# Gates' cumulative sums by split decay logarithms in single-pass products, in a two-layer hybrid token mixer on Trainium2

## What is computed

```python
def gla_chunked(q, k, v, logg, s0, with_output=True):
    g = jnp.cumsum(logg.astype(f32).reshape(b, n, GLA_CHUNK, h, dk), axis=2)
    g_last = g[:, :, -1]
    k_upd = k * jnp.exp(g_last[:, :, None] - g)
    ...
    g_mid = g[:, :, GLA_CHUNK // 2 - 1][:, :, None]
    scores = jnp.einsum('bnihd,bnjhd->bnhij', q * jnp.exp(g - g_mid), k * jnp.exp(g_mid - g))
    scores = jnp.where(mask, scores, 0.0)
    o_intra = jnp.einsum('bnhij,bnjhv->bnihv', scores, v)
    o_inter = jnp.einsum('bnihd,nbhdv->bnihv', q * jnp.exp(g), s_start)

logg_f = jax.nn.log_sigmoid((lr_f @ w_dec_f + b_dec_f).astype(jnp.float32)) / GLA_TAU
```

## Time and profile before

| | |
|---|---|
| median of 3 runs | 1604.45 us (1604.32 to 1606.06) |
| profiled execution | 1607.49 us, its span 1605.7 us, mean granted clock 0.988 |
| TensorE busy | 1541.2 us, 96% of the span |
| VectorE, ScalarE, GpSimd busy | 862.1, 569.0, 594.3 us |
| loop over the tiles, layer 0 | 263.3 to 310.3 us of the span |
| loop over the tiles, layer 1 | 1131.3 to 1166.0 us |

### The profile page before, as it was taken

The page is one execution under the profiler, slowest core; times in us unless marked ns, Lnnn a source line. Parts: engine busy times, 40 slices in busy tenths (PEclk is TensorE's granted clock), DMA queues, the critical chain, the costliest instruction groups (busy, mean ns, idle before and its releaser), DMA issues.

```text
span 1605.7 us, 22916 instructions
## 1 busy us (share of the span) xinstructions
PE 1541.2 (96%) x9056; PEld 1388.4 (86%) x9056; DVE 862.1 (54%) x1316; ACT 569.0 (35%) x916; POOL 594.3 (37%) x309
## 2 busy tenths in 40 slices
PE   5999999999999999999999979999999999999997
PEld 2899999886799999999999858888898888888887
DVE  2576888536646425761466675477756332223237
ACT  4644214426444213441244246432535321322221
POOL 0532211245324524553255223322342444444441
PEclk9999999999999999999999999999999999999999
DMA  9554531355312203122122341563130333323221
GB/s 369 200 167 153 162 125 59 113 173 206 118 52 81 79 26 104 54 79 79 53 80 64 140 162 54 196 198 116 51 136 27 118 108 116 130 91 103 93 83 61
DMA packets 54062, 183.93 MB, mean 115 GB/s; under 512 B 5650, under 2 KB 10642, under 8 KB 51028
## 3 DMA queue, kind: packets, MB, share of 16 engines
q1 hardware_dynamic: 47826, 168.85, 31.3%
q10 hardware_dynamic: 6146, 13.83, 2.5%
HBM read 171.13 MB, written 11.53 MB: 114 GB/s over the span
## 4 chain that ended last, share of the span: by engine, by line
PE 89%; DVE 5%; ACT 2%; DMA 1%; issue 1%; SPq 1%; POOL 1%; ACTq 0%; DVEq 0%; POOLq 0%
PE A L1038 62%; PE A L1292 8%; PE N L1292 4%; PE G L1292 4%; DMA raw<-modw 1%; PE A L1226 1%; PE A L1220 1%; PE G L1195 1%; PE G L1347 1%; PE G L1154 1%; PE A L1188 1%; DVE x L2177 1%; PE N L1138 1%; SPq L892 1%; DVE A L2176 1%
## 5 line engine op out<-in xcount | busy, mean ns | idle before, releaser
L976 POOL TENSOR_TENSOR w_lo<-raw,w_hi 128x1024 fp32r<-128x1024 f32 (+2 forms) x163 | 386.7, 2375 | 654.7 <-ACT w_hi L1374 617.4
L1038 PE MATMUL A<-h_hi,w_hi 128*128 128x512 f32 (+2 forms) x1264 | 414.6, 359 | 15.8 <-POOL h_lo L1021 7.0
L1038 PE MATMUL A<-h_lo,w_hi 128*128 128x512 f32 (+2 forms) x1264 | 405.2, 351 | 0.0
L1038 PE MATMUL A<-h_hi,w_lo 128*128 128x512 f32 (+2 forms) x1264 | 405.1, 351 | 0.0
L1374 ACT ACTIVATE w_hi<-raw 128x1024 fp32r<-128x1024 f32 (+2 forms) x163 | 167.5, 1030 | 372.6 <-PE A L1038 334.5
L1038 PEld LDWEIGHTS A<-h_hi,w_hi 128*128 128x128 f32 x1264 | 235.7, 190 | 55.2 <-issue 12.4
L1038 PEld LDWEIGHTS A<-h_hi,w_lo 128*128 128x128 f32 x1264 | 237.8, 191 | 22.1
L1038 PEld LDWEIGHTS A<-h_lo,w_hi 128*128 128x128 f32 x1264 | 237.8, 191 | 21.6 <-issue 0.5
L1038 PE MATMUL A<-g_hi,w_hi 128*128 128x384 f32 (+2 forms) x480 | 146.9, 349 | 3.8 <-DVE g_lo L1867 2.0
L1038 PE MATMUL A<-g_hi,w_lo 128*128 128x384 f32 (+2 forms) x480 | 145.8, 347 | 0.0
L1038 PE MATMUL A<-g_lo,w_hi 128*128 128x384 f32 (+2 forms) x480 | 145.8, 346 | 0.0
(11 more groups left out here) (313 smaller groups left out, 2625.6 us busy)
## 6 DMA issues: line engine op xcount, KB each, us to landing
raw<-stream SPq DMA_DIRECT2D x150, 512.0 KB, 3.7
mraw<-modv SPq DMA_DIRECT2D x54, 512.0 KB, 4.5
mraw<-modw SPq DMA_DIRECT2D x10, 1024.0 KB, 6.6
raw<-pairs SPq DMA_DIRECT2D x18, 512.0 KB, 4.8
raw<-modw SPq DMA_DIRECT2D x6, 1024.0 KB, 14.7
x<-x_keep ACTq DMA_DIRECT2D x4, 1536.0 KB, 13.7
raw<-stream SPq DMA_DIRECT2D x16, 384.0 KB, 3.1
bg<-modv SPq DMA_DIRECT2D x10, 512.0 KB, 3.8
```

The lines of the kernel that those rows point to most:

```text
L976: pool.tensor_tensor(lo, like_chunk(n, raw[:, n % RAW, 0:WIDTH[n]]), hi.bitcast(F32), ALU.subtract).then_inc(lo_done, 1)
L1038: m = pe.matmul(dst[:, at:at + t1 - t0], a, b[:, k, t0:t1], start=(first and p == 0), stop=(last and p == 2))
```

## The change

The decay logarithms are split too. For each tile ScalarE copies `ls` to `ls_high` in float32r, GpSimd subtracts to get `ls_low`, and `gate` becomes two single-pass products into one sum, `ls_high` and `ls_low` each with `mat_r`, a float32r copy of the constants (made once). There is one buffer of each. The new tensors lie over tensors that are not in use then (`wd`, the first part of `mat`, `mrow`), so all others keep their places. ScalarE makes the first tile's copy ahead of the `four` copies and each further one behind the exponentials of the tile before. GpSimd's subtraction for the next tile stands at this tile's gates, and the weight conversions are placed around it.

The pieces of the diff, in this order: allocation, GpSimd, TensorE at `gate`, ScalarE at `four`, ScalarE at `gate` behind its exponentials.

```diff
+        with ls_low_t:
+            ls_low = sb("ls_low", [P, 512], F32R, stack=ls_low_t)
...
+        with mat_t:
+            mat_r = sb("mat_r", [P, 4 * P], F32R, stack=mat_t)
...
+        with ls_high_t:
+            ls_high = sb("ls_high", [P, 512], F32R, stack=ls_high_t)
...
+                if e[0] == "gate":
+                    tiles = tiles_of(e[1])
+                    at = tiles.index(e[2])
+                    if at == 0 and e[3] == 0:
+                        low_until(PLAN.n0[e] + RING)
+                    elif e[3] and at:
+                        low_until(max(done[0], PLAN.n0[e] + (at if e[1] else max(0, at - 2))))
+                    if at + e[3] < len(tiles) and (e[3] or at == 0):
+                        pool.wait_ge(lshi_ready, nth(e[1], tiles[at + e[3]]) + 1)
+                        pool.tensor_tensor(ls_low[:, :], ls[:, tiles[at + e[3]], :], ls_high[:, :].bitcast(F32),
+                                           ALU.subtract).then_inc(lslo_ready, 1)
                 if e[0] == "fold":
-                    low_until(PLAN.n0[("wout", e[1])])
+                    low_until(max(done[0], PLAN.n0[("wout", e[1])]))
...
-                    read_out(pe, ("z", L, tt))
+                    pe.wait_ge(lslo_ready, nth(L, tt) + 1)
                     for pr in range(2):
-                        m = pe.matmul(G[g][:, pr * 256:(pr + 1) * 256], ls[:, tt, g * KW + pr * P:g * KW + (pr + 1) * P],
-                                      mat[:, g * 256:(g + 1) * 256], start=True, stop=True)
+                        own = slice(g * KW + pr * P, g * KW + (pr + 1) * P)
+                        pe.matmul(G[g][:, pr * 256:(pr + 1) * 256], ls_high[:, own], mat_r[:, g * 256:(g + 1) * 256],
+                                  start=True, stop=False)
+                        m = pe.matmul(G[g][:, pr * 256:(pr + 1) * 256], ls_low[:, own], mat_r[:, g * 256:(g + 1) * 256],
+                                      start=False, stop=True)
...
+                    if nth(L, tt) == 0:
+                        act.wait_ge(consts_in, 16 * 4)
+                        link(act.activation(mat_r[:, :], mat[:, 0:4 * P], ACT.Copy))
+                    if tt == tiles_of(L)[0]:
+                        for t in tiles_of(L):
+                            read_out(act, ("z", L, t))
+                        act.activation(ls_high[:, :], ls[:, tt, :], ACT.Copy).then_inc(lshi_ready, 1)
...
+                    at = tiles_of(L).index(tt) + 1
+                    if g and at < len(tiles_of(L)):
+                        act.activation(ls_high[:, :], ls[:, tiles_of(L)[at], :], ACT.Copy).then_inc(lshi_ready, 1)
```

More of the change, by code:

```diff
@@ L544, in bass_hybrid_block @@
         par = sb("par", [P, DEPTH * PCOLS + 16])
+        ls_low_t, mat_t, ls_high_t = ExitStack(), ExitStack(), ExitStack()
+        with ls_low_t:
+            ls_low = sb("ls_low", [P, 512], F32R, stack=ls_low_t)
         wd = sb("wd", [97, 512])
         mask = sb("mask", [P, 2, P], I32)
+        with mat_t:
+            mat_r = sb("mat_r", [P, 4 * P], F32R, stack=mat_t)
         mat = sb("mat", [P, 4 * P + 2 * P + 2])
@@ L657, in bass_hybrid_block @@
         qk_ready, r_scaled = sem("qk_ready"), sem("r_scaled")
+        lshi_ready, lslo_ready = sem("lshi_ready"), sem("lslo_ready")
         osq_ready, orstd_ready, yg_ready, yhi_ready, ylo_ready = (
```

## The result

The change made the kernel slightly slower: 1607.99 us median (20 runs) against 1605.26 us for the kernel before in the same comparison (20 runs). The ratio is 1.0016, 95% interval 1.0010 to 1.0023, that is +2.6 us (+1.6 to +3.7): the ratio lies within the 0.2% that were called "same" ahead, its interval reaches 0.23%. Predicted were +2.15 (+0.5 to +4.5) and 1606.6 us; of the 1.4 us between that and 1607.99, 0.8 come from the median of the kernel before, which stood at 1604.45 after three runs and stands at 1605.26 after twenty.

A forecast was written before the change was run, and what follows sets the result against it. Layer 0 was taken as bound by two nearly equal chains, TensorE's 7.79 us and a ScalarE-VectorE loop of 7.6; layer 0's +3.15 and layer 1's -1.0 summed to +2.15, 1606.6 us, range +0.5 to +4.5.

The forecast's parts named there:

- The lock between VectorE and GpSimd: GpSimd's subtraction runs between VectorE's two products of a tile, making the second 1.15 later in every tile but the last.
- Layer 0, tile by tile: Layer-0 loop: shifts of each tile's first exponential, -1.15, then +1.15, +1.0, +1.15, +1.0, summing to +3.15 us.
- Tile 2: earlier by one and a half gates: Layer 0, second tile's first exponential: comes 1.15 us earlier through the cheaper gates.
- Layer 1: Layer-1 loop: first two tiles about even; third has 2.3 - 1.15 less in VectorE's way, of which -1.0 us is kept.
- Gates: TensorE's gates: eight single-pass products take 0.95 instead of 1.73 us, saving 0.78 per tile, 7.8 us of queue over ten tiles.
- gates not cheaper: Rival: gate products cost 0.216 per pair-of-types product, so layer 0 +4.7, layer 1 -0.7, total +4.0, 1608.5 us; chance 0.04.
- TensorE's idle of 1.7 us: Layer 0, each of the last three tiles: TensorE idle some 1.7 us (8.75 - 7.01) before score or mean-square products.
- no collision: Rival: subtraction slips in before or beside VectorE's first product; layer 0 gains 1.1, layer 1 2.3, giving 1601.0 us; chance 0.11.

The follow-up runs named there:

- e5: Kernel after, with GpSimd's subtraction, from the third tile's logarithms on, waiting until VectorE's two products of the current tile are done; ratio 1.0008.
- e4: Kernel before, with only layer 1's first output-projection weight conversion on GpSimd moved early, to the second tile's gate; ratio 0.9986.
- e1: Kernel after without GpSimd's ten subtractions, each second gate product repeating the rounded half, so the low part is left out; ratio 0.9989.
- e2: Kernel after with the float32 gates of before, the subtraction kept and waited for though unread, ScalarE's copy of the constants left out; ratio 1.0017.
- e7: Kernel after with subtractions from the third tile on moved to VectorE, and ScalarE's square behind the weight conversion in some tiles; ratio 0.9994.
- e10: Kernel before with layer 1's early weight conversion, the square behind the conversion, and GpSimd's second layer-1 conversion held back; 1603.74 us, ratio 0.9997.
- e11: Kernel after with subtractions from the third tile on VectorE, the later square, and GpSimd's second layer-1 weight conversion held back; ratio 1.0002.

## Why the prediction held, point by point

The mechanism, a subtraction that takes its turn between VectorE's two products, came as predicted. The size came right in part by luck: in each layer two terms were too large, one of them a gain and one a price, and their errors nearly cancel.

- **The lock between VectorE and GpSimd: right in kind and size.** Taken were 1.15 to 1.2 for the subtraction, between the two products; measured is 1.14 (295.79 - 294.65), and L2049 at 1.75. The Trainium skill (SBUF — State Buffer, "Who interferes with whom") says that two-input VectorE work and GpSimd's reads shut each other out for whole instructions; e5 shows it in one tile, where the product with a PSUM input ran through at 0.68 and the one with two SBUF inputs took 1.33.
- **Layer 0, tile by tile.** The first exponentials stand at 265.71, 273.66, 282.42, 291.04 and 299.65, in before at 265.60, 272.53, 280.54, 288.11 and 295.90. Counted from the first `four` product, against before: tile 2 -0.39, tile 3 +0.63, tile 4 +1.38, tile 5 +2.43, tile 6 +3.25, end +3.35. Predicted: -1.15, 0, +1.0, +2.15, +3.15. The end is right through **two errors that cancel**. The step that failed is "Tile 2: earlier by one and a half gates": the first tile's gates gave nothing, since the DFT products behind them wait for the last low part of the `four` stage (255.34 in after, again 6.95 us behind the first `four` product, 0.55 us idle). And each later tile added less than said: +1.02, +0.75, +1.05, +0.82 instead of +1.15, +1.0, +1.15, +1.0.
- **Layer 1:** predicted -1.0, measured -0.83. But its parts were mis-sized, and again the errors cancel. Taken were 2.3 for the conversion moved away and 1.15 back for the subtraction, both in the third tile; the early conversion alone gives 1.44 (e4), and the split gates beside it cost 0.61 (44.91 - 44.30). In the third tile the subtraction holds L2069 by only 0.35 us (1.04 instead of 0.69); it costs more in the first, which I had as even: the second tile's subtraction stands in the first tile's products there (L2049 1.78 us), and VectorE's masked copy starts 13.48 us behind the first `four` product instead of e1's 12.72.
- **Gates:** 0.95 per tile was predicted; the eight records start 0.12 apart except the first (288.95 to 289.89, so 1.06 with the last's share). That is 0.67 saved a tile, not 0.78. The rival "gates not cheaper", +4.0, wasn't the case; e2, its counterpart, shows +3.1, since cheap gates were worth 0.54 us and not 1.9.
- **TensorE's idle of 1.7 us** in each late tile: its busy time there is 7.74 of 8.61, so 0.87. But the ends of its records are modelled. e7 gives a better measure: with the same products it needs 7.09 us a tile when it never waits, against the 7.01 that I had taken. By that, 1.5 of after's 8.61 us are idle, near the forecast.
- **Rival "no collision", 1601.0:** e1 is that case and gave 1603.37, 2.0 below its own before where 3.45 were forecast. It fell short in both layers, 0.21 in layer 0 for 1.1 and 1.91 in layer 1 for 2.3. In layer 0 the first tile's saving is lost as said for tile 2, and behind it the round trip of ScalarE and VectorE (7.55 us a tile) doesn't contain the gates. In layer 1 the moved conversion alone gives 1.44 (e4) where 2.3 were taken.

## What to carry to other kernels

Where two chains of a loop are nearly equal, work moved off one engine pays only if its replacement stands in a gap of the other chain: in layer 0 the same subtraction cost 3.6 us between two VectorE products and nothing on VectorE itself in a wait of 0.7 us, while in layer 1, with a held product ahead of it, TensorE waited 0.77 us for it. A saving must also be followed to the next waiter; here the first tile's was lost at once to a low part, and nearly all the others to the round trip, until GpSimd's weight conversion was out of VectorE's way too. When an edit pays, look in the rows for the reason: the later square paid by what it moved ahead of itself. And split a change into its parts: the reordering in layer 1 that came along with it was worth more than the cheaper gates.

## What the runs showed of the hardware that I had not expected

- In the rows here GpSimd and VectorE take turns, one instruction each, when both have locked work queued: in after the subtraction began when L2048 ended and L2049 when the subtraction did (294.65, 295.79). So the position in GpSimd's queue decides who pays. In e10, where a pass was held back, it was the next tile's first product: 3.26 us instead of 1.3.
- An operation that waits for the lock is recorded as busy. VectorE became 13.4 us busier with the same 1316 instructions; a page's busy share overstates an engine that is locked out.
- TensorE's granted clock fell inside a loop after short waits: in e7, idle 1.65 and 0.77 us around 1.16 us of work, it was at 0.53 in the next 3.6 us and the gate records stood 0.21 us apart instead of 0.12; in e11, with one wait of 0.48 there, it stayed at 1.00.
